# Index scores as pairs of heads on two halves of the array's rows, with the forget-gate products dealt between the pairs

## What is computed

```python
h = rmsnorm_2(x, norm_mix)
hq, hf, hi, hg, sq, sk, sv, iq, ik, iw, mq = split_in(h @ w_in)

# index scores: 8 heads of 64, which choose 128 keys for each query
s = jnp.einsum('bqhd,bsd->bqhs', iq, ik)
score = jnp.einsum('bqh,bqhs->bqs', iw, jax.nn.relu(s))
score = jnp.where(visible[None], score, -jnp.inf)
_, idx = lax.top_k(score, topk)

# recurrence: hf is the forget gate's logit, hq the query
log_f = jnp.logaddexp(jnp.log(lb), jnp.log1p(-lb) + jax.nn.log_sigmoid(hf))
k = (1.0 - lb) * jax.nn.sigmoid(-hf)
qf = jax.nn.silu(hq)
```

## Time and profile before

| | us |
|---|---|
| median of 3 runs | 1558.2 |
| lowest and highest | 1557.84, 1559.09 |
| the profiled execution | 1558.86 |
| its span | 1557.1 |
| TensorE busy | 1533.1 |
| VectorE busy | 879.5 |
| ScalarE busy | 626.4 |

### The profile page before, as it was taken

How to read it: one execution, slowest core, us unless ns; L and a number is a source line. 1 busy time by engine, 2 the same in 40 slices (tenths; PEclk the granted TensorE clock), 3 DMA queues, 4 the chain that set the end, 5 groups by cost and what they waited for, 6 DMA issues and landing times. The chain is left out here.

```text
span 1557.1 us, 20519 instructions
## 1 busy us (share of the span) xinstructions
PE 1533.1 (98%) x7830; PEld 1289.6 (83%) x7830; DVE 879.5 (56%) x1356; ACT 626.4 (40%) x870; POOL 15.5 (1%) x21
## 2 busy tenths in 40 slices
PE   7999999999999999999999999989999999999999
PEld 7898778888888888888888868989888888888887
DVE  5454565355456877777533788878764434444322
ACT  6442444232245544444333556664553422222210
POOL 0000000000000000000000000000000000000000
PEclk9999999999999999999999999999999999999999
DMA  9313211322323133232323222020103223232232
GB/s 359 131 55 108 102 55 55 108 92 96 109 108 135 55 108 108 81 108 81 135 108 135 64 91 99 28 78 33 55 28 108 94 95 108 81 108 85 104 108 81
DMA packets 23372, 151.01 MB, mean 97 GB/s; under 512 B 2595, under 2 KB 3107, under 8 KB 6284
## 3 DMA queue, kind: packets, MB, share of 16 engines
q1 hardware_dynamic: 23228, 150.01, 27.0%
q10 hardware_dynamic: 80, 0.13, 0.0%
HBM read 147.87 MB, written 2.13 MB: 96 GB/s over the span
## 5 line engine op out<-in xcount | busy, mean ns | idle before, releaser
L1128 DVE TENSOR_TENSOR w_lo<-raw,w_hi 128x2048 fp32r<-128x2048 f32 x112 | 256.6, 2291 | 342.0 <-ACT w_hi L627 341.8
L1841 PE MATMUL bank<-h_hi,w_hi 128*128 128x512 f32 x1096 | 431.1, 393 | 0.5 <-DVEq L1201 0.2
L1843 PE MATMUL bank<-h_hi,w_lo 128*128 128x512 f32 x1096 | 427.0, 390 | 0.0
L1842 PE MATMUL bank<-h_lo,w_hi 128*128 128x512 f32 x1096 | 426.6, 389 | 0.0
L627 ACT ACTIVATE w_hi<-raw 128x2048 fp32r<-128x2048 f32 x123 | 235.0, 1910 | 319.5 <-PE bank L1843 304.4
L1841 PEld LDWEIGHTS bank<-h_hi,w_hi 128*128 128x128 f32 x1096 | 205.5, 187 | 43.7 <-DVE w_lo L1128 0.9
L1843 PEld LDWEIGHTS bank<-h_hi,w_lo 128*128 128x128 f32 x1096 | 205.3, 187 | 43.7
L1842 PEld LDWEIGHTS bank<-h_lo,w_hi 128*128 128x128 f32 x1096 | 205.5, 188 | 41.5
L1841 PE MATMUL bank<-a_hi,w_hi 128*128 128x512 f32 x352 | 136.9, 389 | 0.0
L1842 PE MATMUL bank<-a_lo,w_hi 128*128 128x512 f32 x352 | 136.9, 389 | 0.0
L1843 PE MATMUL bank<-a_hi,w_lo 128*128 128x512 f32 x352 | 136.9, 389 | 0.0
(11 more groups left out here) (308 smaller groups left out, 2051.9 us busy)
## 6 DMA issues: line engine op xcount, KB each, us to landing
raw<-weights SPq DMA_DIRECT2D x128, 1024.0 KB, 4.8
toep<-bias_scratch SPq DMA_DIRECT2D x8, 448.0 KB, 4.7
x<-xT SPq DMA_DIRECT2D x2, 1024.0 KB, 12.5
x_tok<-x_tok SPq DMA_DIRECT2D x1, 2048.0 KB, 13.4
mem2T<-mem2T SPq DMA_DIRECT2D x2, 1024.0 KB, 4.7
outT<-x SPq DMA_DIRECT2D x8, 256.0 KB, 4.2
lead<-lead SPq DMA_DIRECT2D x2, 512.0 KB, 5.4
lead<-lead SPq DMA_DIRECT2D x1, 1024.0 KB, 8.1
```

Of the source, the lines that this page charges most:

```text
L1128: nc.vector.tensor_tensor(w_lo[PLACE[m]][:, :], raw[m % 2][:, :], w_hi[PLACE[m]][:, :].bitcast(F32), ALU.subtract).then_inc(lo_ready, 1)
L1841: nc.tensor.matmul(o, lh, rh, start=first, stop=False)
L1842: nc.tensor.matmul(o, lh, rl, start=False, stop=False)
L1843: return nc.tensor.matmul(o, ll, rh, start=False, stop=last)
```

## The change

It does the index scores in twelve pairs of heads. The even head uses rows 0 to 63 of the array, the odd head rows 64 to 127, each with its own copy of the keys in the one buffer `ik`; the zero halves and their two memsets are gone. Behind each pair TensorE does two of the 24 products of `hf` tiles 1 to 3. The transposes of `km_tok` follow after the last pair, in banks 4 and 5.

ScalarE rounds `hf` load 1 before it copies `iw`, `hq` load 0 after the fourteenth relu, and `hq` load 1 after the first two `abs`. VectorE runs `between_scores` after each pair of sums: half a split, a normalization, the causal add of the first query block, or one selection round. After the last pair it does the two other causal adds, `hf` tile 3, the split of `hq` load 1 and rounds 3 to 9. From the log on everything is as it was.

```diff
--- before.py
+++ after.py
-    tiles("turn_km", 2, (2, 3))
+    tiles("turn_km", 2, (4, 5))
...
-        ik = [at(f"ik{s}", AR + (40 + 2 * s) * K, [S]) for s in range(2)]
+        ik = at("ik", AR + 40 * K, [S])
...
             pool.wait_ge(w_used, FIRST["mem_v2"] + 1)
-            nc.gpsimd.memset(ik[0][64:P, :], 0.0).then_inc(ik_padded, 1)
-            pool.wait_ge(ik_padded, 1)
-            nc.gpsimd.memset(ik[1][0:64, :], 0.0).then_inc(ik_padded, 1)
-            pool.wait_ge(ik_padded, 2)
...
-            nc.scalar.dma_start(ik[1][64:P, :], ik[0][0:64, :]).then_inc(ik_odd_in, 16)
+            nc.scalar.dma_start(ik[64:P, :], ik[0:64, :]).then_inc(ik_odd_in, 16)
             head_root(MT * SAH)
+            round_w(FIRST["hf"] + 1)
             ready(("iw", 0))
...
                 frees(("idx", w), nc.scalar.activation(relu[w % 2][:, 0:keys], B(("idx", w))[:, 0:keys], ACT.Relu))
+                if w == 13:
+                    round_w(FIRST["hq"])
...
-            round_w(FIRST["hf"] + 1)
             for odd in range(2):
...
             for m in range(2):
-                round_w(FIRST["hf"] + m + 2)
+                if m:
+                    round_w(FIRST["hq"] + 1)
...
-            frees(("ik", 0), nc.vector.tensor_tensor(ik[0][0:64, :], B(("ik", 0))[0:64, :], rms[0:64, :], ALU.mult))
+            frees(("ik", 0), nc.vector.tensor_tensor(ik[0:64, :], B(("ik", 0))[0:64, :], rms[0:64, :], ALU.mult))
...
+            def hide_later(i):
+
+                cut = sel[:, i, P * i:P * (i + 1)]
+                link(nc.vector.tensor_tensor(cut, cut, causal[:, :], ALU.add))
+
+            def between_scores(pair_):
+
+                if pair_ in (1, 2):
+                    split_part(FIRST["hf"] + 1, pair_ - 1)
+                if pair_ in (7, 8):
+                    split_part(FIRST["hq"], pair_ - 7)
+                if pair_ in (3, 5, 9):
+                    t = {3: 0, 5: 1, 9: 2}[pair_]
+                    ready(("hf", t))
+                    normal("hf", t, lf[:, t * S:(t + 1) * S])
+                if pair_ == 4:
+                    dve.wait_ge(relu_used, IDXH + 2)
+                    hide_later(1)
+                if pair_ in (6, 10, 11):
+                    r = {6: 0, 10: 1, 11: 2}[pair_]
+                    top_keys(r, r + 1)
...
+                if w % 2:
+                    between_scores(w // 2)
             dve.wait_ge(relu_used, len(IDX))
-            for i in range(1, TT):
-
-                link(nc.vector.tensor_tensor(sel[:, i, P * i:P * (i + 1)], sel[:, i, P * i:P * (i + 1)], causal[:, :],
-                                             ALU.add))
...
-            for m in range(2):
-                if m == 0:
-                    split_w(FIRST["hf"] + 1)
-                for t in (2 * m, 2 * m + 1):
-                    ready(("hf", t))
-                    normal("hf", t, lf[:, t * S:(t + 1) * S])
-                split_w(FIRST["hf"] + m + 2)
-                top_keys(5 * m, 5 * m + 5)
+            for i in (2, 3):
+                hide_later(i)
+            ready(("hf", 3))
+            normal("hf", 3, lf[:, 3 * S:4 * S])
+            split_w(FIRST["hq"] + 1)
+            top_keys(3, 10)
...
-            pe.wait_ge(ik_padded, 2)
-            for w_, (i, h) in enumerate(IDX):
-                claim(("idx", w_))
-
-                done(("idx", w_), nc.tensor.matmul(B(("idx", w_))[:, 0:P * (i + 1)], iq[:, h // 2, i * P:(i + 1) * P],
-                                                   ik[h % 2][:, 0:P * (i + 1)], start=True, stop=True))
+            for w_ in range(0, len(IDX), 2):
+                for e in range(2):
+                    claim(("idx", w_ + e))
+                for e in range(2):
+                    i, h = IDX[w_ + e]
+                    rows_ = slice(64 * e, 64 * e + 64)
+                    done(("idx", w_ + e), nc.tensor.matmul(
+                        B(("idx", w_ + e))[:, 0:P * (i + 1)], iq[rows_, h // 2, i * P:(i + 1) * P],
+                        ik[rows_, 0:P * (i + 1)], start=True, stop=True))
+                for p_ in (KT + w_, KT + w_ + 1):
+                    t, kt = divmod(p_, KT)
+                    ld, key, cs = FIRST["hf"] + t // 2, ("hf", t), slice(t % 2 * P, (t % 2 + 1) * P)
+                    if kt == 0:
+                        weights(ld)
+                        claim(key)
+                    ins = product(B(key)[:, :], w(ld, 1)[:, kt, cs], w(ld, 0)[:, kt, cs], h_hi[:, kt, :], h_lo[:, kt, :],
+                                  kt == 0, kt == KT - 1)
+                    if kt == KT - 1:
+                        done(key, ins)
             turn_heads("turn_km", km_tok, M)
-            for t in range(1, 4):
-                ld = FIRST["hf"] + t // 2
-                weights(ld)
-                claim(("hf", t))
-                done(("hf", t), feature_tile(B(("hf", t)), ld, t % 2, *H))
```

More of the change, by code:

```diff
@@ L443, in build @@
         padded = sem("padded")
-        iw_rows, ik_odd_in, ik_padded = (sem(x_) for x_ in ("iw_rows", "ik_odd_in", "ik_padded"))
+        iw_rows, ik_odd_in = sem("iw_rows"), sem("ik_odd_in")
         half_rms = sem("half_rms")
@@ L1615, in top_keys @@
                         link(nc.vector.tensor_scalar(scores, scores, TAKEN, NEG, ALU.not_equal, ALU.mult))
-            for m in range(2):
-                if m == 0:
-                    split_w(FIRST["hf"] + 1)
-                for t in (2 * m, 2 * m + 1):
+            def hide_later(i):
[8 more added lines that the diff above has]
+                    t = {3: 0, 5: 1, 9: 2}[pair_]
                     ready(("hf", t))
                     normal("hf", t, lf[:, t * S:(t + 1) * S])
-                split_w(FIRST["hf"] + m + 2)
-                top_keys(5 * m, 5 * m + 5)
+                if pair_ == 4:
[4 more added lines that the diff above has]
+                    top_keys(r, r + 1)
+            for w, (i, h) in enumerate(IDX):
+                keys = P * (i + 1)
+                wait_free(("idx", w))
+                if w:
+                    dve.wait_ge(relu_used, w)
+                nc.vector.scalar_tensor_tensor(out=sel[:, i, 0:keys], in0=relu[w % 2][:, 0:keys],
+                                               scalar=iw[:, i, h:h + 1], in1=sel[:, i, 0:keys], op0=ALU.mult,
+                                               op1=ALU.add).then_inc(relu_used, 1)
+                if w % 2:
+                    between_scores(w // 2)
+            dve.wait_ge(relu_used, len(IDX))
+            for i in (2, 3):
[4 more added lines that the diff above has]
+            top_keys(3, 10)
             for m in range(2):
```

## The result

The changed kernel took 1560.97 us (median of 19 runs, 1559.11 to 1563.10), the kernel before 1558.37 us (19 runs beside them, 1557.84 to 1560.78). The ratio is 1.0016, 95% interval 1.0010 to 1.0022: 2.6 us slower.

The account below looks back on a forecast made before the run. The prediction took TensorE, busy 98% of the span, as the bound. Its terms, −3.0 on TensorE, +3.8 of wait and +1.5 of clock, gave +2.3 us: 1560.5 in terms of the median, range 1556.0 to 1562.6.

Parts of the forecast that it names:

- TensorE's gain: Index scores: paired heads and a removed split wait, less small losses, bring TensorE to `hq` 3.0 us sooner, at 935.5.
- `sfx` at 949.5: VectorE before `sq`: seven rounds instead of five behind the split of `hq` load 1 start `sfx` 1.2 us later.
- The wait for `tok`: TensorE at `sq` tile 3, needing bank 0: waits 4.2 us in place of 0.45, resuming near 970.15.
- VectorE has slack there: Beyond `sq` tile 3, up to 990: no TensorE wait for `z`, so the shift is carried to the end.
- the gain stays: Rival at `sq` tile 3: bank 0 is free by 966, `sfx` some 4 us sooner; 1555.2 us, chance 0.10.
- The clock: Around the wait before dense `sq` matmuls: one fall to half rate, costing 1.5 us, bounds 0 and 3.4.
- The slower rival: Clock stays at 1.2 GHz twice as long, costing 3.3 us instead of 1.5: 1562.3 us, chance 0.20.
- The price of the fall of the earlier trace: Second block, 1050.72 to 1054.13, granted clock 0.50: half of 3.41 us, 1.7 us of work, given away.
- The sum: Whole kernel: −3.0 on TensorE, +3.8 of wait, +1.5 of clock, together +2.3 us.
- The range: Whole kernel's time: 1556.0 to 1562.6 us, leaving out most of the faster case and the slower case's upper tail.

Follow-up runs that it names:

- full-row run: Changed kernel with its dealing and new order, but each index matmul over all 128 rows, with zero halves and memsets: 1563.10 us, ratio 1.0034.
- pairs alone: Kernel before with pairs of heads on two halves of the rows and nothing else, no products dealt between them: 1558.81 us, ratio 1.0003.
- Two rounds fewer: Changed kernel with five selection rounds instead of seven behind the split of `hq` load 1, two moved to the list's end: 1558.84 us, ratio 1.0002.
- the rounding ahead of copies and `abs`: Changed kernel with ScalarE's rounding of `hq` load 1 in front of the four `kmT` copies and two `abs`: 1558.37 us, ratio 1.0000.
- filled run: Changed kernel with 16 unread matmuls of 512 columns into bank 3 in front of `sq` tile 3: 1558.57 us, ratio 1.0002.
- bank 3 alone: Changed kernel with `sq` tile 3 in PSUM bank 3 instead of bank 0: 1563.21 us, ratio 1.0033.
- room and bank 0: Changed kernel with four selection rounds moved out of VectorE's way, `sq` tile 3 staying in bank 0: 1558.48 us, ratio 1.0000.

## Why the prediction was right

The forecast was 1560.5 us, the measured time 1560.97. By its steps:

- **TensorE's gain, 3.0 us foreseen, 2.9 measured.** Pairs of 0.95 and 1.39 us, the `iw` wait of 0.33, no wait for the split of `hf` load 1, and no TensorE wait for VectorE inside the stage. The full-row run confirms the size of it from the other side, 2.9 us. What the prediction did not say is that the pairs alone bring next to nothing (0.2 us of the stage): the dealing takes away the relu and sum limit, the pairs then cut TensorE's own time, and only where they are wide.
- **`sfx` at 949.5, measured 949.73, 949.43 without the late start.** Both halves of the reason were tested apart. Two rounds fewer, or the rounding ahead of copies and `abs`, each brought it to where the logarithm holds it, and the wait fell by 1.4 and 1.6 us.
- **The wait for `tok`, 4.2 us until 970.15, measured 3.66 until 970.35 (970.05 without the late start).** The end is right. The wait is 0.5 us shorter because it is counted from 966.4 (without the late start) and not from 965.9. Of this, 0.16 is that the profile counts from the last matmul's end (966.40 + 0.28) and not from the next one's turn (966.40 + 0.12), and 0.07 the smaller gain. The other 0.25 lies between the start of `hq` and tile 3, 30.65 us for 21.76 + 8.64; the forecast had no wait for the split in front of `sq`, which TensorE, now early, meets at 957.80. How much of the 0.25 it makes was not taken apart.
- **"VectorE has slack there" was wrong as it stood**, and did no harm to the number: at TensorE's real arrival nothing waits for VectorE's copies, but 3 us earlier there are two ends, not one. The rival "the gain stays" had named only bank 0 and a `sfx` 4 us sooner. It came true with less on `sfx` (1.5 us), another bank, and two more rounds out of VectorE's way later on.
- **The clock, 1.5 us foreseen.** This term was mis-sized: 2.4 us, both by the filled run's median and between the two profiled executions. The stretch covered 5.46 us of work, not the 3.41 of the earlier trace rows. The slower rival had put its border at 4.6 us of work, and the profiled execution, with 5.46 us, did come out 3.06 us above that of before (1561.92 for 1558.86); the median stayed below. The Trainium skill (TensorE: Matmul & The Clock Gate, HAM oscillation — how this bites in real kernels) says that an idle gap puts TensorE back to half rate. The trace agrees, with 0.50 beside the 3.66 us wait, and the runs give the price.
- **The price of the fall of the earlier trace rows.** The prediction took half of 3.41 us, 1.7 us, as given away there. Less was lost. The kernel before, with the fall, takes 1067.25 − 1049.55 = 17.70 us from the end of the wait for `pT` to the end of the next wait for `mix`. The filled run, without a fall, takes 1067.38 − 1050.32 = 17.06 (first the kernel before, then the filled run):

```profile
1067.25 0.66 PE L2007 MATMUL bank<-vm,pT 128*128 128x64 f32 x4 [0.50 <-DVE mix L1305]
```

```profile
1067.38 0.66 PE L2023 MATMUL bank<-vm,pT 128*128 128x64 f32 x4 [1.08 <-DVE mix L1304]
```

The difference is 0.64 us; the wait for `mix` alone shrank by 0.58. Behind tile 3 the rows show no wait before level 0, and there the clock cost 2.4 us.

- **The sum.** The profiled executions differ by 3.06 us: 0.30 of late start, 0.70 of later start of tile 3, 2.4 of clock, less 0.3 for a wait near 1135 that shrank from 1.36 to 1.02 us. The medians differ by 2.6. Half rate does not last equally long in every execution: six of the 19 had a mean granted clock of 0.996 and took 1560.97 to 1563.10 us, and six had 0.999, which leaves room for about one stretch of 3.4 us, and took 1559.11 to 1560.92. So the closeness of 1560.5 to the median of 1560.97 is in part luck: the forecast priced one stretch of fixed length, shorter than in the profiled execution. The range, 6.6 us wide, would also have held no change at all.

## What to carry to other kernels

When one engine is made faster, list every buffer that it will ask for until the next place where it stood, and date each release on the new schedule: taking away the wait that the profile shows may only uncover a second one of the same length a few microseconds on. Work dealt into one stage comes back as idle time if a link of another engine's program order still ties the next stage to the stage's end; so move the link, or leave the waiting engine less to do behind it. And a wait of TensorE in front of dense work can cost as much again in clock (2.4 and 4.0 us beside waits of 3.6 here), but only as far as no later wait takes it up (0.64 us near 1050); matmuls that nobody reads, put into the wait, measure that share.

## What the runs showed of the hardware

- In or just behind each of the three unfilled waits of 3.6 to 3.7 us the granted clock fell: in the changed kernel for 6.83 us, with bank 3 alone for 10.24 us (both stretches are shown above), with full rows for 3.41 us, from 0.3 us after the wait had ended at 972.33:

```profile
972.62:976.03 3.41, 3.41 (x18) 3.41 (x18) 3.31 (x7) 0.39 (x2) 0.00 (x0) 0.50 0.00 0
```

- Waits of 1.7 to 2.3 us were followed by half rate in some executions and not in others. The wait of 2.3 us with two rounds fewer, which ended at 968.44, was followed by it (the stretch below). The run with room and bank 0 waited 2.3 us at the same place, and its mean granted clock was 1.000. The wait of 1.7 us for `pT` near 1050 stands in all twelve profiled executions; six were at half rate in the 3.4 us behind it, the kernel before and the changed one among them, and six were not. The same program can go either way: the mean granted clock of the changed kernel's 19 executions runs from 0.996 to 0.999. What decides it was not found.

```profile
969.10:972.51 3.41, 3.41 (x18) 3.41 (x17) 3.31 (x7) 0.02 (x1) 0.00 (x0) 0.50 0.00 0
```

- With pairs alone the clock also fell inside the index stage, where no wait of TensorE is longer than 0.73 us:

```profile
911.43:914.84 3.41, 3.41 (x12) 1.33 (x12) 2.89 (x6) 2.39 (x6) 0.00 (x0) 0.50 0.00 0
```

- A pair on two halves of the rows is far from half price when it stands alone between full-row products: 0.95 to 1.39 us from product to product, and the second product behind it is 0.34 us after the first instead of 0.23. Twelve such pairs saved 2.9 us against 24 matmuls over full rows, 1.8 of them in the four pairs of 512 columns, 1.0 in those of 384 and 0.1 in those of 256.
